# One stage fewer: the last cached rows and the sample's retention run inside the output projection

## The reference, cut to what matters

```
z = rms_norm(x) @ w_in                 # -> rq rk rv rg dq dk dv dg
# group A, prompt: chunked retention, 16 chunks of 128, state S (128 x 128 per head)
# group A, sample: S_new = g * S + k^T v ; o = q S_new          (8 rows, 4 heads)
# group B, prompt: a = softmax(q1 k1) - lam * softmax(q2 k2), causal ; o = a v
# group B, sample: the same over 32 cached pages of 128 keys plus the row's own key
u = concat(rms(o_ret) * silu(rg), rms(o_diff) * silu(dg))
y = x + u @ w_out                      # 2048 prompt rows, 8 sample rows
```

## Time and profile before

| | us |
|---|---|
| median of 3 runs | 2116.42 (2111.71 to 2120.24) |
| the profiled execution, whole | 2115.8 |
| its span, first to last instruction | 2113.8 |
| mean granted PE clock | 0.905 |

### The profile page before, as it was taken

One profiled execution on the slowest core, in us unless ns is written; L12 is line 12 of the kernel. 1 busy time (PEld: TensorE's weight loads), 2 busy tenths in 40 slices (PEclk: granted clock), 3 DMA queues, 4 the chain that ended last, 5 costly groups with the idle time before them and its releaser, 6 DMA issues. The chain is left out here.

```text
span 2113.8 us, 28626 instructions
## 1 busy us (share of the span) xinstructions
PE 1682.2 (80%) x8308; PEld 1259.1 (60%) x8308; DVE 1120.2 (53%) x1972; ACT 730.8 (35%) x1939; POOL 1024.6 (48%) x1912
## 2 busy tenths in 40 slices
PE   6778888978889766776888778888788877439998
PEld 2256656655657455664666556666666666307887
DVE  2555565755666345566755767455554553361211
ACT  3232222322322223444444445455554544211100
POOL 4747685766666356564646555454254441140000
PEclk9989899989999878988999889999999996769999
DMA  7752656647455332213341334112200000244442
GB/s 289 250 168 76 198 175 199 201 144 236 151 188 189 110 110 65 65 55 123 118 115 36 95 105 125 55 41 82 78 16 16 16 11 11 69 129 130 131 137 71
DMA packets 168773, 241.93 MB, mean 114 GB/s; under 512 B 15314, under 2 KB 82011, under 8 KB 168611
## 3 DMA queue, kind: packets, MB, share of 16 engines
q1 hardware_dynamic: 163218, 223.38, 33.7%
q0 software_dynamic: 5408, 16.85, 2.0%
HBM read 211.89 MB, written 28.28 MB: 114 GB/s over the span
## 5 line engine op out<-in xcount | busy, mean ns | idle before, releaser
L589 POOL TENSOR_TENSOR s_ring<-s_ring,s_q_row 128x1024 f32<-128x1024 f32 x128 | 316.1, 2485 | 81.6 <-DMA s_ring<-in_cache_k 78.9
L1563 PE MATMUL s_z<-g_w_hi,s_h_hi 128*128 128x512 f32 x512 | 235.3, 460 | 53.6 <-DVE s_gate L1457 35.5
L1062 PE MATMUL s_z<-g_w_hi,s_h_hi 128*128 128x512 f32 x512 | 232.8, 455 | 15.6 <-DVE s_h_lo L964 11.8
L596 DVE TENSOR_REDUCE s_scores<-s_ring 128x16 f32<-128x1024 f32 x128 | 153.3, 1212 | 114.8 <-POOL s_ring L589 114.8
L1565 PE MATMUL s_z<-g_w_hi,s_h_lo 128*128 128x512 f32 x512 | 214.0, 418 | 0.0
L1564 PE MATMUL s_z<-g_w_lo,s_h_hi 128*128 128x512 f32 x512 | 213.4, 417 | 0.0
L1319 ACT ACTIVATE s_p<-s_sc,s_neg_max 128x1024 f32<-128x1024 f32 (+4 forms) x192 | 166.9, 870 | 128.3 <-DVE s_neg_max L1484 73.2
L1064 PE MATMUL s_z<-g_w_hi,s_h_lo 128*128 128x512 f32 x512 | 209.5, 409 | 0.0
L1063 PE MATMUL s_z<-g_w_lo,s_h_hi 128*128 128x512 f32 x512 | 209.2, 409 | 0.0
L1611 PE MATMUL s_o<-s_v,s_aT 128*128 128x128 f32 x1088 | 164.1, 294 | 25.5 <-ACT s_aT L1300 25.5
L1611 PEld LDWEIGHTS s_o<-s_v,s_aT 128*128 128x128 f32 x1088 | 156.4, 207 | 45.2 <-ACT s_aT L1300 33.8
(11 more groups left out here) (242 smaller groups left out, 3643.4 us busy)
## 6 DMA issues: line engine op xcount, KB each, us to landing
s_ring<-in_cache_k SPq DMA_DIRECT2D x256, 256.0 KB, 2.8
s_ring<-in_cache_v SPq DMA_DIRECT2D x256, 256.0 KB, 2.8
w_raw<-in_w_in SPq DMA_DIRECT2D x8, 2048.0 KB, 8.9
s_w_raw<-in_w_in SPq DMA_DIRECT2D x56, 256.0 KB, 4.6
s_u_in<-u_scratch SPq DMA_DIRECT2D x17, 512.0 KB, 4.0
x_in<-in_x_prompt SPq DMA_DIRECT2D x16, 512.0 KB, 4.8
s_table<-c_rope_ret SPq DMA_DIRECT2D x64, 128.0 KB, 3.2
u_scratch<-s_gate POOLq DMA_DIRECT2D x32, 256.0 KB, 2.7
```

The lines of the kernel that those rows point to most:

```text
L589: pool.tensor_tensor(slot[:], slot[:], bc(R.q_row[:].unsqueeze(1), [P, 2, 512]), ALU.mult).then_inc(R.keys_times_q, 1)
L596: dve.tensor_reduce(R.scores[r % 2][:, 2 * j:2 * j + 2, :], R.slot(("k", r, j))[:].rearrange("p i (s f) -> p i s f", f=DH), AX, ALU.add).t ...
L1062: pe.matmul(b[:], hi[:, c, :], g.w_hi[:, wc, :], start=(wc == 0), stop=False)
L1563: pe.matmul(z_bank[:], hi[:, c, :], g.w_hi[:, wc, :], start=(wc == 0), stop=False)
```

## The change

`diff_stage` loses the rows: no ring, no row bank in PSUM, none of the row steps. The PSUM bank that this frees becomes a second `z` bank, used in turn, so `project` waits for the `gate_z` of two tiles before. It gets 8 raw weight buffers: a head's 8 chunks are loaded at t = 2, each once its buffer has been split, and split four and four around the head's boundary. In slots 64 to 67, where nothing is projected any more, ACT and POOL split `w_out` in 16 pieces of 128x512, into the place of `hT`.

`final_stage` takes the place of stages 4 and 5. Its unit is a quarter of an output tile, called a slot here too: 12 of the 48 products of 128x512. There are 68 slots for 17 tiles. Woven into them are rows 5 to 7 with a ring of 5 (`FINAL_PLAN`), and the sample's retention in 16 steps in slots 6 to 21. The 17th tile is the sample itself, turned from `o` instead of being read from HBM. `x` is loaded straight into the `y` buffers, of which there are three, and ACT issues the stores of `y`.

```diff
-WRAW = 3
+WRAW = DC
-        z_bank = psum("z", 512)
+        z_bank = [psum(f"z{i}", 512) for i in range(2)]
-                if half == 0 and s >= 1:
-                    pe.wait_ge(z_gated, s)
+                if half == 0 and s >= 2:
+                    pe.wait_ge(z_gated, s - 1)
...
-                row_keys_dve(dve, R, s)
-                row_steps_dve(dve, g, R, s)
                 if s < TILES:
                     gate_z(s)
...
+            def split_out_weights(n):
+                act.wait_ge(w_loaded[n % DC], 16 * (NH + n // DC))
+                act.wait_ge(half_low, 2 * TILES)
+                act.copy(out_part(g.wo_hi, n), w_raw[n % DC][:]).then_inc(wo_high, 1)
...
+PARTS = 4
+FINAL_PLAN = [
+    (list(range(0, 14)), 14, [20, 21, 22, 23]),
+    (list(range(15, 29)), 29, [35, 36, 37, 38]),
+    (list(range(30, 44)), 44, [50, 51, 52, 53]),
+]
+FINAL_ROWS = Rows(5, 5, FINAL_PLAN, OUT_SLOTS)
...
+            for q in range(OUT_SLOTS):          # SP
+                n, part = q // PARTS, q % PARTS
+                while sent < min(R.due[q] + R.depth - 1, len(R.order)):
+                    row_load(sp, io, g, R, sent)
+                    sent += 1
+                if part == 2:
+                    if 2 <= n + 2 < NT:
+                        load_u(n + 2)
+                    if n + 1 < OUT_TILES:
+                        load_x(n + 1)
...
+            for q in range(OUT_SLOTS):          # PE
+                n, part = q // PARTS, q % PARTS
+                products(n, part)
+                for job in turns_at(q):
+                    turn(*job)
...
+                if halves_at(q):
+                    sample_step(*halves_at(q))
+                row_values_pe(pe, R, q)
+                row_steps_pe(pe, g, R, q)
```

More of the change, by code:

```diff
@@ L1343, in _ @@
                 if 1 <= k < NH and t == 0:
-                    for x in range(WRAW, DC):
+                    for x in range(DC // 2, DC):
                         split_w(k, x)
@@ L1756, in _ @@
+            store_y(NT)
+            for i in range(Y_RING):
+                act.wait_ge(stored[i], 16 * len(range(i, OUT_TILES, Y_RING)))
         @block.gpsimd
@@ L1802, in _ @@
+            for q in range(OUT_SLOTS):
+                row_keys_pool(pool, R, q)
+                row_store(pool, io, R, q)
+                if q == AT_OUTPUT:
+                    pool.wait_ge(ms_ready, 1)
+                    chain.link(pool.tensor_scalar(ms[:], ms[:], 1.0 / P, EPS, ALU.mult, ALU.add))
+                    rsqrt_steps(pool, chain, rstd[:], ms[:], nw_t[:], nw_h[:])
+                    pool.sem_inc(rstd_ready, 1)
+            pool.wait_ge(R.row_stored, 32 * R.count)
         @block.vector
@@ L1977, in _ @@
+            add_x(NT)
         @block.tensor
         def _(pe):
-            pe.sem_inc(product, 1)
-            pe.sem_inc(turned, 1)
-            pe.sem_inc(y_ready, 2)
-            def turn(n, k, waits):
-                pe.wait_ge(u_loaded[k], waits)
-                for c in range(DC):
-                    last = pe.transpose(turn_bank[2 * k + c // 4][:, (c % 4) * P:(c % 4 + 1) * P],
-                                        u_in[k][:, c * P:(c + 1) * P], g.ident[:])
-                last.then_inc(turned, 1)
@@ L2029, in build, with turn @@
-def build(nc, io, stages=(1, 2, 3, 4, 5)):
+            def turn(n, half):
+                if n < NT:
+                    pe.wait_ge(u_loaded[n % 2], 16 * (n // 2 + 1))
+                else:
+                    pe.wait_ge(u_ready, 1)
+                if n >= 1:
+                    pe.wait_ge(u_split, 2 * n - 1 + half)
+                r = rows[n]
+                for c in range(4 * half, 4 * half + 4):
+                    src = u_in[n % 2][:, c * P:(c + 1) * P] if n < NT else o[:, c, :]
+                    last = pe.transpose(turn_bank[half][:, (c % 4) * P:(c % 4) * P + r], src, g.ident[0:r, 0:r])
+                last.then_inc(turned, 1)
@@ new lines, in products @@
+            def products(n, part):
+                r = rows[n]
+                if part == 0:
+                    if n >= 2:
+                        pe.wait_ge(y_ready, n - 1)
+                    pe.wait_ge(u_split, 2 * n + 1)
+                elif part == 2:
+                    pe.wait_ge(u_split, 2 * n + 2)
+                for c in (2 * part, 2 * part + 1):
+                    hi, lo = u_hi[n % 2][:, c, 0:r], u_lo[n % 2][:, c, 0:r]
+                    for x, w, first, end in ((hi, w_hi, c == 0, False), (hi, w_lo, False, False),
+                                             (lo, w_hi, False, c == DC - 1)):
+                        for half in range(2):
+                            last = pe.matmul(y_bank[2 * (n % 2) + half][0:r, :], x,
+                                             w[:, c, 512 * half:512 * half + 512], start=first, stop=end)
+                if part == PARTS - 1:
+                    last.then_inc(product, 1)
```

599 lines of the change are left out of this document (286 added, 313 removed).

## The result

| | before | after |
|---|---|---|
| median, us (lowest to highest, runs) | 2116.28 (2111.71 to 2120.24, 4) | 2160.39 (2156.75 to 2164.08, 4) |
| profiled execution / its span | 2115.8 / 2113.8 | 2156.98 / 2154.9 |
| stage 3, from 743.80 | 1092.6 | 995.9 |
| the rest | 61.4 + 216.0 | 415.2 |

The ratio is 1.0209 with a 95% interval of 1.0178 to 1.0241. The change makes the kernel 2.1% slower; I had forecast 2.4% faster. Stage 3 came out as forecast (996 against 993). The final stage took 415 us where I had 325, and that is nearly the whole miss.

What follows compares the result with a forecast made beforehand. Stage 5 was taken as bound by PE, stage 4 by a chain of small steps, stage 3 in between; 743.8 + 993 + 325 = 2062 us of span, predicted 2065 us, range 2030 to 2105.

Steps and rivals of the forecast that it cites:

- gaps between heads: Stage 3, slot 15 to slot 16: eight raw buffers and absent rows bring all three gaps to 20 us, gaining 23.4.
- Rival 3: Stage 3: cached rows aren't what lengthens early heads; only 50 of 100 us won, 2115 us, no change; chance 0.10.
- `w_out` term: Stage 3, slots 64 to 67: 16 ACT casts and 16 POOL subtractions cost 0; uncovered, 10 us of ACT.
- rival 4: Stage 3: second `z` bank or even split does nothing; 23 us at most, inside the forecast, no separate chance.
- term of the rows: Final stage: cost given to cached rows 5 to 7, 87 us, including 50 us of page waits.
- sample's steps: Final stage: DVE's and PE's halves meet in 16 slots, with state stores and loads; 0 to 20 us, taken as 8.
- starved value slots: Final stage, slots 20-23, 35-38, 50-53: PE waits for value pages paced by SP's issues, 50 us together.
- Rival 2: Final stage: DMA saturates, loads land in 6 us instead of 2.8; slower than before, 2131 us; chance 0.07.
- That is below 256, but the plan isn't even.: Final stage: SP's 230 us fit below PE's 256, but dense value slots add 50 us of page waits.
- one of my own signs of being wrong: Final stage: PE waiting for `u_in` or the sample's steps by more than 20 us in all would refute the forecast.
- The short row steps: 3.: Final stage: the short steps of cached rows 5 to 7 add 3 us to PE's work.
- Twelve starved slots can leave PE at the lower level when work is dense again: 0 to 25 us, I take 8.: Final stage: after waits for value pages PE's granted clock may stay near the lower level; 8 us taken.

## Why the prediction was wrong

**Stage 3 was right in its terms, but for one.** Forecast and measured gain, in us:

| term | forecast | measured |
|---|---|---|
| first head, slots 0 to 4 | 14 | 41.5 - 28.1 = 13.4 |
| first head, slots 4 to 15 | 33.3 | 174.7 - 141.9 = 32.8 |
| second, third, last head | 21.8 + 5.5 + 2 | 23.5 + 7.0 + 3.5 |
| gaps between heads | 23.4 | 27.8 |
| `w_out` in the last slots | 0 | -12.6 |
| before the first slot (stage 2 ended sooner) | 0 | 1.1 |
| all | 100 | 96.7 |

The last head had shown what a head without rows costs, and that held. Rival 3 is refuted. The `w_out` term is the one wrong step here: "ACT and POOL have little else" looked at busy time, where ACT is 36 of 102 us busy. But the casts stand in ACT's queue ahead of a square that DVE's combination of the map waits for, in a chain of single steps that ends in PE. I had named a price of 10 us if uncovered. That the sum came within 4 us is partly luck: the other terms gave 9 us more than forecast, which hid this one, and the trace has the shorter of the two tails. Of rival 4 half came true: the second `z` bank is worth nothing, the raw buffers are worth 19 us.

**The final stage.** The term of the rows was 87 us and measured 178.6:

| part of the rows' cost | forecast | measured |
|---|---|---|
| waits for value pages | 50 | 42.0 |
| products of values (L671) | 22.8 | 33.5 |
| row steps, busy and waits | 3 | 5.9 + 22.1 |
| waits for `u` behind pages on SP | 0 | 45.2 - 14.0 = 31.2 |
| slower products, less clock | 8 | 305.0 - 33.5 - 5.9 - 226.2 = 39.4 |
| sample's steps, beyond the kernel without rows | 0 | 4.5 |

The starved value slots, to which I gave all the thought, were nearly right in size: from first to last value product they took 45, 38 and 30 us for each four, where I had 39, 39 and 30 from the start of the first slot to the last landing. SP issued pairs through nearly all of them without a pause, as forecast, and they lengthened and shortened with its time a pair, so the mechanism stands too. Rival 2 had the direction, but not the reason: pages landed in 3.1 us and not in 6, and fewer bytes changed nothing. (It also counted 56 key slots, where the plan has 42, so its 16 us should be 12.) The steps that failed:

1. "That is below 256, but the plan isn't even." I looked for the unevenness in value slots only and put the waits for `u` at nothing; they were 31.2 us behind the start, one of my own signs of being wrong. I had asked what is queued behind a waiting PE, but not what is queued ahead of `u` in SP's list: pairs issued one after another (9.2 + 1.8 us), query loads that wait for the last key product (13.6 + 1.8) and page loads that wait for the ring (4.8).
2. "The short row steps: 3." They measured 5.9 us of work and 22.1 of waits. These are a ping-pong of PE and DVE, four times a row. I counted PE's instructions and not its waits.
3. "Twelve starved slots can leave PE at the lower level when work is dense again: 0 to 25 us, I take 8." The loss follows all stops together, not the twelve starved slots alone. It came out at 39, over my upper bound.
4. The range. Its upper end for the final stage, some 350 us, let two terms grow, the clock and the sample's steps, and left the waits for `u` and in the row steps at nothing. More stops also mean more time at the lower clock, so these terms grow together.

The Trainium skill, "DMA: Bandwidth & Descriptors", section "Issuing engines are not separate DMA queues", says that to start DMAs on several engines only saves sequencer time, which is usually small. Here moving 14 loads to another engine's queue took 31 us of waits away, and 19 us of time. The 14 loads themselves need 0.43 us each; what they lost was their place in line, some behind SP's own time for a run of pairs, more behind an instruction of SP that waited. For the other finding the trace agrees with the Trainium skill, "SBUF — State Buffer", section "Who interferes with whom": an operation of VectorE with two SBUF inputs contends with GpSimd's reads, and a reduction doesn't. The combination went from 1288 to 2067 ns, while in the final stage the sum over the key pairs (L596), a reduction of one SBUF tile, took 1213 ns in the mean beside GpSimd's products.

## What to carry to other kernels

Before moving work from a stage with slack into one that PE bounds, list for each in-order queue what stands behind every instruction that can wait, DMA queues included; a load whose buffer is free is late all the same if loads ahead of it wait, or are simply many. Price the stops of PE with the clock: here each 100 us of short stops cost 35 to 65 more. And a low busy share of an engine doesn't make an insertion free, if the bound is a chain that passes through that engine.

## What the runs showed of the hardware that I had not expected

- Stops of 2.6 us on average, 40 in 420 us, brought the granted clock from 0.97 to 0.80, and one of 1.99 us after dense work brought it from 1.00 to 0.50.
- A page load of 256 KB landed in 3.1 us (median), one of 512 KB in 5.3, one of 128 KB in 2.6. Two loads of 256 KB, the second issued 0.5 us behind the first, are there sooner than one of 512 KB, though that one read the same page twice. A load of 64 partitions took SP longer to issue than one of 128, 0.47 us against 0.33.
- The same instructions at the end of stage 3 took 115 us in three traces and 123 in seven, PE busy for 65 to 67 us against 70 to 71.
- At 195 GB/s and at 135 GB/s the stage took the same time. A DMA share of 0.60 said nothing about the bound.
- VectorE's small product for the sample (L1903, two SBUF inputs) took 3.24 us once and 1.20 in its other runs. GpSimd's product beside it ran from 1780.97 to 1783.32, and it ended 1.07 us behind that. The sums (L596) kept 1.21 and 1.20:

```profile
1780.03 1.21 DVE L596 TENSOR_REDUCE s_scores<-s_ring 128x16 f32<-128x1024 f32 x1
1781.15 3.24 DVE L1903 TENSOR_TENSOR s_v_own<-s_z,s_own_row 8x1024 f32<-8x1024 f32 x1
```
